# Second attention of a two-layer encoder: each head's four projection pieces in three PSUM banks instead of one

## What is computed

```python
down = u @ w_down
c_q = _rms_norm(down[..., :MLA_Q_LORA], q_norm_w)
c_kv = _rms_norm(down[..., MLA_Q_LORA:MLA_Q_LORA + MLA_KV_LORA], kv_norm_w)
...
q = (c_q @ w_uq).reshape(B, S, MLA_HEADS, MLA_NOPE + MLA_ROPE)
...
kv = (c_kv @ w_ukv).reshape(B, S, MLA_HEADS, MLA_NOPE + MLA_V)
...
for qb in range(S // Q_BLOCK):
    q0 = qb * Q_BLOCK
    n_keys = q0 + Q_BLOCK
    s = (jnp.einsum('bqhd,bkhd->bhqk', q_nope[:, q0:n_keys], k_nope[:, :n_keys])
         + jnp.einsum('bqhr,bkr->bhqk', q_rope[:, q0:n_keys], k_rope[:, :n_keys])).astype(F32) * scale
    p = _masked_softmax(s, _chunk_mask(q0, n_keys)[None, None])
    outs.append(jnp.einsum('bhqk,bkhe->bqhe', p.astype(v.dtype), v[:, :n_keys]))
```

## Time and profile before

| what | us |
| --- | --- |
| median of 3 runs (2898.30 to 2898.93) | 2898.34 |
| the profiled execution's own time | 2890.08 |
| its span, first to last instruction | 2888.4 |
| PE busy in it | 2649.1 (92%) |
| DVE busy | 1557.7 (54%) |
| ACT busy | 1168.0 (40%) |
| the sixteen heads, from about 1560 to 2051 us | 491 |

### The profile page before, as it was taken

One profiled execution on the slowest core, in us unless ns is written; L12 is line 12 of the kernel. 1 busy time (PEld: TensorE's weight loads), 2 busy tenths in 40 slices (PEclk: granted clock), 3 DMA queues, 4 the chain that ended last, 5 costly groups with the idle time before them and its releaser, 6 DMA issues. The chain is left out here.

```text
span 2888.4 us, 36971 instructions
## 1 busy us (share of the span) xinstructions
PE 2649.1 (92%) x12454; PEld 2173.6 (75%) x12454; DVE 1557.7 (54%) x2537; ACT 1168.0 (40%) x2071; POOL 436.6 (15%) x440
## 2 busy tenths in 40 slices
PE   3899989879999999999997888888799999999997
PEld 2677777757788888887766777777577888888886
DVE  4577777747754443443765566566376323232346
ACT  2366656534512213123454666666246122131224
POOL 0000000001110010051143544444110000000000
PEclk8999999989999999999999999999899999999999
DMA  8233333263342241321341111111633111111123
GB/s 319 77 98 101 109 91 109 78 234 93 102 138 88 80 131 51 117 80 57 89 132 23 36 30 25 35 29 35 226 95 88 59 50 51 44 51 51 44 88 102
DMA packets 325470, 255.20 MB, mean 88 GB/s; under 512 B 40647, under 2 KB 290806, under 8 KB 324350
## 3 DMA queue, kind: packets, MB, share of 16 engines
q1 hardware_dynamic: 309550, 195.26, 23.2%
q0 software_dynamic: 14736, 50.34, 5.6%
q10 hardware_dynamic: 1088, 8.39, 0.7%
HBM read 216.17 MB, written 33.59 MB: 86 GB/s over the span
## 5 line engine op out<-in xcount | busy, mean ns | idle before, releaser
L1832 PE MATMUL PA<-U,W 128*128 128x512 f32 x3840 | 950.2, 402 | 68.4 <-DVE H L1723 51.0
L1832 PEld LDWEIGHTS PA<-U,W 128*128 128x128 f32 x3840 | 725.9, 191 | 239.2 <-DVE H L1723 37.3
L782 ACT ACTIVATE W<-raw 128x1024 fp32r<-128x1024 f32 (+2 forms) x262 | 260.0, 994 | 817.5 <-PE PA L1832 389.8
L1832 PE MATMUL SC<-U,W 128*128 128x512 f32 x2064 | 482.3, 392 | 10.3 <-DMA U<-attention_out 6.5
L1832 PEld LDWEIGHTS SC<-U,W 128*128 128x128 f32 x2064 | 387.8, 188 | 96.9 <-DMA U<-attention_out 7.1
L1832 PE MATMUL PA<-H,W 128*128 128x512 f32 x1536 | 359.1, 392 | 3.2 <-DVE W L1244 3.2
L1832 PE MATMUL SC<-H,W 128*128 128x512 f32 x1536 | 355.3, 390 | 0.0
L1244 DVE TENSOR_TENSOR W<-raw,W 128x1024 fp32r<-128x1024 f32 x232 | 286.9, 1237 | 103.5 <-ACT W L782 102.3
L1832 PEld LDWEIGHTS PA<-H,W 128*128 128x128 f32 x1536 | 288.3, 188 | 64.3 <-DVE W L1244 3.6
L1832 PEld LDWEIGHTS SC<-H,W 128*128 128x128 f32 x1536 | 288.1, 188 | 60.7 <-issue 1.0
L580 POOL DMA_DIRECT2D ada<-in_ada_w x80 | 57.9, 724 | 873.3 <-DVE acc L1258 869.8
(11 more groups left out here) (245 smaller groups left out, 3097.8 us busy)
## 6 DMA issues: line engine op xcount, KB each, us to landing
raw<-in_ffn_w SPq DMA_DIRECT2D x160, 512.0 KB, 4.0
ada<-in_ada_w POOLq DMA_DIRECT2D x80, 512.0 KB, 4.5
U<-attention_out SPq DMA_DIRECT2D x4, 3584.0 KB, 17.5
raw<-in_da_w_qkv SPq DMA_DIRECT2D x24, 512.0 KB, 5.1
ada_first<-in_ada_w ACTq DMA_DIRECT2D x4, 2048.0 KB, 18.1
H<-H SPq DMA_DIRECT2D x32, 256.0 KB, 5.1
attention_out<-ostage SPq DMA_DIRECT2D x32, 256.0 KB, 2.9
raw<-in_da_w_o SPq DMA_DIRECT2D x16, 512.0 KB, 3.9
```

The source lines that it names most:

```text
L782: nc.scalar.activation(W[:, slot, 0, 0:kt * P], raw[:, slot, 0:kt * P], ACT.Copy).then_inc(w_hi, 1)
L1832: ins = mm(bank, W[:, slot, a, kt * P:(kt + 1) * P], moving(b, kt)[:, cols], start=kt == first and (a, b) == SPLIT[0], stop=kt == last and ...
```

## The change

Piece 1 of each next head now goes to VB, piece 3 to the upper bank of SC0; pieces 0 and 2 stay in PA0. For the first head, whose pieces are made ahead of the loop, nothing changes. The waits before each piece are rewritten to what last used its bank, and `values1` of a head's first half gets a wait in front of it until piece 1 has been taken out of VB. Line numbers of the changed kernel are higher by 1, and by 6 after `proj1`.

```diff
+        def piece_bank(piece): return (PA[0][:, :], VB[:, :], PA[0][:, :], SC[0][:, HALF:S])[piece]
...
                     if s == 0 and not is_first(h):
-                        copy_piece(p, h, 3, PA[0])
+                        copy_piece(p, h, 3, piece_bank(3))
                     if s in (2, 4, 6) and proj:
-                        copy_piece(1 - p, h + 1, s // 2 - 1, PA[0])
+                        copy_piece(1 - p, h + 1, s // 2 - 1, piece_bank(s // 2 - 1))
...
                     if s == 0 and not is_first(h):
-                        lo_piece(p, h, 3, PA[0])
+                        lo_piece(p, h, 3, piece_bank(3))
                     if s in (2, 4, 6) and proj:
-                        lo_piece(1 - p, h + 1, s // 2 - 1, PA[0])
+                        lo_piece(1 - p, h + 1, s // 2 - 1, piece_bank(s // 2 - 1))
...
                 pe.wait_ge(w_lo, g0 + kv + 2 * hi + 1)
+                if is_first(h) and piece >= 2:
+                    pe.wait_ge(a1["qk_evac"], piece - 1)
                 if not is_first(h):
-                    pe.wait_ge(a1["qk_evac"], 4 * h + piece)
-                elif piece >= 2:
-                    pe.wait_ge(a1["qk_evac"], piece - 1)
+                    if piece % 2 == 0:
+                        pe.wait_ge(a1["qk_evac"], 4 * h - 1 + piece)
+                    elif piece == 1:
+                        pe.wait_ge(a1["o_fin"], 2 * h - 2)
+                    else:
+                        pe.wait_ge(a1["p_ready"], NQ * h - 1)
...
                     if proj and s % 2:
-                        proj1(g0, 2 * i, h + 1, s // 2, PA[0])
+                        proj1(g0, 2 * i, h + 1, s // 2, piece_bank(s // 2))
                     if s == 4:
                         inverses1(h, 0, evacuated(h, I_EARLY - 2), t1_bank(I_EARLY, p))
+                        if proj:
+                            pe.wait_ge(a1["qk_evac"], 4 * h + 6)
                         values1(h, 0)
```

## The result

| | us |
| --- | --- |
| before, median of 4 (2893.29 to 2898.93) | 2898.32 |
| changed kernel, median of 4 (2916.45 to 2932.78) | 2928.49 |
| ratio, 95% interval | 1.010, 1.0083 to 1.0116 |
| profiled execution: own time, span | 2925.56, 2923.9 |

A forecast was written before the change was run, and what follows sets the result against it. PE bounds the stage, only just, with a loop of PE, VectorE and ScalarE nearly as tight. Profiled: 2890.1 + 13.2 (waits) + 13.2 (clock) = 2916.5; median: 2898.3 + 26.4 = 2924.7 us, range 2904 to 2938.

The forecast's parts named there:

- Piece 1 wins nothing: Steps 3 to 4: piece 1's wait of 1.56 goes, but `inverses1` stays and waits about 1.6; gain 0.
- The wait in front of `values1`, 1.39 a head: Step 4: `values1` waits until piece 1 has left VB; loss 1.39 us a head.
- Piece 3 keeps 0.51: Steps 7 to 0: piece 3's wait of 1.13 goes, and 0.51 us a head is gained.
- Waits alone, +13.2: Fifteen heads: the `values1` loss less piece 3's gain, 15 x (1.39 - 0.51) = +13.2 us.
- The clock, +25 less 11.8: New step 4 pauses bring clock falls in most heads, +25; the old falls, 11.8, go; net +13.2 us.
- (b): Rival: the clock never falls in the heads; 13.2 - 11.8 = +1.4, 2899.7 us; chance 0.10.
- (a): Rival: waits as read, but step 4 lets the clock fall only as often as before; +13.2, 2911.5 us; chance 0.16.
- (c): Rival: the clock falls for the long kind in every head; +48, 2947 us; chance, with cases near it, 0.07.
- (d): Rival: faster, the clock holds and step 7 keeps piece 3's full 1.13; -7.9, 2890.4 us; chance 0.05.
- (e): Rival: faster by the whole wait, other banks hiding each evacuation in the heads; -40.4, 2857.9 us; chance 0.02.

The follow-up runs named there:

- the two clean kernels: Changed kernel with useless products in both step 4 pauses, 2896.5 us; changed kernel with piece 1 taken out early and products ahead of `inverses1`, 2879.1 us.
- the fourth experiment: The changed kernel, waits kept, with eleven useless products a head in the two pauses of step 4: 2896.5 us, ratio 1.0005.
- the fill experiment: The kernel before, with useless products into VB in its two pauses, six ahead of piece 1 and four ahead of piece 3: 2883.6 us, ratio 0.9961.

## Why the prediction was right, and where it was off

- **Piece 1 wins nothing**: right. The chain to `inverses1` did not move, and its wait grew from 0.29 to 1.54 (about 1.6 was said).
- **The wait in front of `values1`, 1.39 a head**: right; 1.40 between the two clean kernels.
- **Piece 3 keeps 0.51**: right; 0.47 with piece 3 alone. The turn of block 0 and `inverses1` in step 0 wait 0.35 and 0.17 in the fourth experiment, where 0.3 to 0.5 was said.
- **Waits alone, +13.2**: right. Clean spans of 30.77 against 29.86 give 15 x 0.91 = 13.7.
- **The clock, +25 less 11.8**: the mechanism was right, the size was low. This is the term that was mis-sized. The fourteen spans of the changed kernel hold 461.5 - 14 x 30.77 = 30.7 us of falls, some 32 for fifteen heads, where the prediction took 25 because it let skipped heads and long falls cancel. No head was skipped, and nine of fifteen falls were long. The price of a long one was set too high, at twice 1.58 = 3.16: by the spans it is 2.3 to 2.9, and 1.4 to 1.6 for a short one. What was taken off, 11.8, was right (11 to 13 in the fill experiment). Net it is 20 instead of 13.2, in the profiled execution; the sum of 2916.5 for it came out 2925.6. Besides the clock, the last head, which the sum left out, is 2.2 us longer between its two `inverses1`, with 6.0 us of slow clock there instead of 2.0. Between the medians the miss is 4 us, less than the 16 by which the changed kernel's own runs differ, so that closeness is in part luck.
- **Rivals.** (b), a clock that never falls, is what the filled kernel gives, 2896.5 where 2899.7 was worked out; the changed kernel itself is not that case. (a) gave 2911.5 and (c) 2947; the result lies between. With piece 1 alone, thirteen of fourteen spans had (c)'s long fall. (d) and (e) did not happen. The rule of the Trainium skill behind (e) ("Perfetto Trace Analysis", Matmuls: rotate groups through different banks) is not refuted in general: with VectorE's chain shortened as well, the same three banks, with piece 0 in VB in place of piece 1, gave 1.4%. In VectorE's old order they gave 0.1%.

The Trainium skill's case of a kernel that cycles through PSUM banks with brief idle times of PE, and a clock that goes up and down with them ("TensorE: Matmul & The Clock Gate", A second HAM failure mode), is told of a kernel in bf16 and fits what the traces of this one in float32 show: 15 falls in the changed kernel, none in the spans once its pauses were filled, 28 to 32 us between the two.

## What to carry to other kernels

Before a wait is taken away, ask which chain holds the engine next: here a pause of 1.56 moved by two instruction groups and nothing was won, and shortening that chain was worth 1.2% between two kernels with the same layout of banks. A shared bank is best given to the piece that leaves it before its owner comes back; one that is taken out after the owner has come makes a new wait in the owner's way. And count TensorE's pauses at two prices: what they last, and the slow clock behind them.

## What the runs showed that was not expected

- The slow clock was worth more than the waits: 20 us net of the 35.5 between the profiled executions. Eleven useless products a head made the changed kernel 28 to 32 us faster, and ten a head made the kernel before 11 to 13 us faster.
- How often the clock falls is not a matter of one pause's length. Ahead of piece 1, about 1.6 us idle with large products on both sides brought one fall in fourteen spans of the kernel before and four with piece 3 alone. Ahead of `inverses1`, 1.54 us idle with transposes behind it brought nine and ten (piece 1 out early, and the other layout). They came in four or five heads in a row, with three heads between that had the same pauses and no fall. And the pauses of step 7, 0.80 and 1.13, that brought six falls before brought none with piece 1 alone, where the clock fell in step 4 of every head instead. Why the same pauses act so differently in two kernels was not settled.
